# Two token blocks of a delta rule's inverse: each step of both issued back to back on TensorE

## What is computed

```python
m = jnp.where(strict, jnp.einsum('bhncd,bhnsd->bhncs', k_beta, kc) * decay, 0.0)
lmat = m + jnp.eye(CHUNK, dtype=m.dtype)
rhs = jnp.concatenate([v_beta, k_beta * jnp.exp(gc)[..., None]], axis=-1)
sol = lax.linalg.triangular_solve(lmat, rhs, left_side=True, lower=True, unit_diagonal=True)
```

## Time and profile before

| | us |
|---|---|
| median of 3 runs | 905.12 |
| the three runs | 903.41, 905.12, 905.43 |
| profiled execution: its time | 902.75 |
| profiled execution: its span | 901.1 |
| TensorE busy in the span | 882.1 |
| VectorE busy | 554.5 |
| ScalarE busy | 294.9 |

### The profile page before, as it was taken

The page is one execution under the profiler, slowest core; times in us unless marked ns, Lnnn a source line. Parts: engine busy times, 40 slices in busy tenths (PEclk is TensorE's granted clock), DMA queues, the critical chain, the costliest instruction groups (busy, mean ns, idle before and its releaser), DMA issues.

```text
span 901.1 us, 13501 instructions
## 1 busy us (share of the span) xinstructions
PE 882.1 (98%) x4615; PEld 705.7 (78%) x4615; DVE 554.5 (62%) x978; ACT 294.9 (33%) x598; POOL 72.7 (8%) x138
## 2 busy tenths in 40 slices
PE   9999999899999999999999999999999999898998
PEld 7887766688888888888888888888787776567877
DVE  6267557365877777777643343497788373774645
ACT  6245475523322222222210011263340213444710
POOL 0010000000010011000001100000000000000000
PEclk9999999999999999999999999999999999999999
DMA  8767433254766555556565566578456222221554
GB/s 277 239 211 226 139 121 113 97 161 139 238 200 195 186 186 191 195 196 197 196 189 187 189 197 199 180 263 266 145 169 192 95 74 92 71 94 47 186 184 145
DMA packets 53862, 154.74 MB, mean 172 GB/s; under 512 B 9628, under 2 KB 15020, under 8 KB 53688
## 3 DMA queue, kind: packets, MB, share of 16 engines
q1 hardware_dynamic: 24496, 75.84, 26.7%
q0 software_dynamic: 19008, 69.21, 23.7%
q10 hardware_dynamic: 10312, 9.06, 3.2%
HBM read 149.60 MB, written 4.49 MB: 171 GB/s over the span
## 4 chain that ended last, share of the span: by engine, by line
PE 89%; DMA 4%; DVE 3%; ACT 2%; issue 2%; POOLq 0%; SPq 0%; ACTq 0%; DVEq 0%
PE bank L716 77%; DMA HI<-wstream 3%; PE bank L1193 1%; PE bank L1171 1%; PE bank L891 1%; PE bank L877 1%; DVE LO L1736 1%; DMA RAW<-wstream 1%; PE bank L1085 1%; PE bank L1102 1%; PE bank L901 1%; ACT SQO L1669 1%; PE bank L1182 1%; PE bank L757 0%; PE bank L1041 0%
## 5 line engine op out<-in xcount | busy, mean ns | idle before, releaser
L716 PE MATMUL bank<-GH,HI 128*128 128x512 f32 x708 | 286.8, 405 | 0.0
L716 PE MATMUL bank<-GH,LO 128*128 128x512 f32 x708 | 275.8, 390 | 0.0
L716 PE MATMUL bank<-GL,HI 128*128 128x512 f32 x708 | 275.4, 389 | 0.0
L1736 DVE TENSOR_TENSOR LO<-RAW,HI 128x1024 fp32r<-128x1024 f32 x86 | 105.2, 1223 | 109.5 <-DMA HI<-wstream 107.5
L716 PEld LDWEIGHTS bank<-GH,HI 128*128 128x128 f32 x708 | 133.3, 188 | 36.7 <-issue 9.1
L716 PEld LDWEIGHTS bank<-GH,LO 128*128 128x128 f32 x708 | 133.0, 188 | 28.4
L716 PEld LDWEIGHTS bank<-GL,HI 128*128 128x128 f32 x708 | 133.4, 188 | 23.1
L698 POOL DMA_DIRECT2D HI<-wstream x132 | 70.1, 531 | 804.3 <-PE bank L716 786.2
L1441 ACT ACTIVATE YC<-AB,PAR 128x512 f32<-128x512 f32 x44 | 36.0, 817 | 140.7 <-DVE AB L1923 140.7
L716 PE MATMUL bank<-AH,HI 128*128 128x512 f32 x176 | 68.5, 389 | 0.0
L716 PE MATMUL bank<-AL,HI 128*128 128x512 f32 x176 | 68.5, 389 | 0.0
(11 more groups left out here) (322 smaller groups left out, 1156.1 us busy)
## 6 DMA issues: line engine op xcount, KB each, us to landing
RAW<-wstream SPq DMA_DIRECT2D x135, 512.0 KB, 3.7
HI<-wstream POOLq DMA_DIRECT2D x132, 512.0 KB, 4.9
X<-x_t SPq DMA_DIRECT2D x8, 256.0 KB, 7.5
NCB<-out_t ACTq DMA_DIRECT2D x8, 256.0 KB, 3.6
out_t<-X ACTq DMA_DIRECT2D x8, 256.0 KB, 5.6
XR<-out_t ACTq DMA_DIRECT2D x8, 256.0 KB, 4.2
out_t<-XR SPq DMA_DIRECT2D x7, 256.0 KB, 3.2
EG<-out_t ACTq DMA_DIRECT2D x1, 1024.0 KB, 4.8
```

Of the source, the lines that this page charges most:

```text
L716: mm = pe.matmul(out, a, b, start=(first and n == 0), stop=(last and n == 2))
L1736: dve.tensor_tensor(LO[:, u % RING, :], RAW[:, u % RING, :], HI[:, u % RING, :].bitcast(F32), ALU.subtract).then_inc(unit_split, 1)
```

## The change

The groups that `_prepare` hands to `_spread` are other ones. Before, nearly each group held one step of one block, so that fills stood behind each step. After, a group holds the same step of both blocks of the pair, one behind the other, and the fills that stood behind each stand behind both. At level 4 Z and X form one group, and X at level 5 and Y at level 6 form one, with both blocks' X ahead of both blocks' Y. A pair thus has eight groups in place of sixteen. The set of items is the same, and no function of an engine is changed.

```diff
+def _both(b, *steps):
+
+    return [(what, (x, l)) for what, l in steps for x in (b, b + 1)]
+
+
 def _prepare(b, fills):
...
-    steps = [[("Y", (x, 4))] for x in (b, b + 1)] + [[("Z", (x, 4)), ("X", (x, 4))] for x in (b, b + 1)]
-    steps += [[(what, (x, l))] for l in LEVELS[1:] for what in ("Y", "Z", "X") for x in (b, b + 1)]
-    steps += [[("W", b)], [("W", b + 1)]]
+    steps = [_both(b, *level) for level in ([("Y", 4)], [("Z", 4), ("X", 4)], [("Y", 5)], [("Z", 5)],
+                                            [("X", 5), ("Y", 6)], [("Z", 6)], [("X", 6)])]
+    steps.append([("W", b), ("W", b + 1)])
     return inputs + _spread(steps, fills)
```

## The result

The changed kernel takes 898.4 us in the median (10 runs, 897.11 to 901.88) against 904.0 us for the kernel before (10 runs, 901.94 to 905.43), a ratio of 0.9949 with a 95% interval of 0.9935 to 0.9963. The profiled execution takes 897.82 us (span 896.1) where its own sum gave 898.95. A second comparison gave 898.35 us against 902.22 and a ratio of 0.9955 (0.9940 to 0.9970). Of all runs in this document three stood far apart from the others of their kernels (1444 and 3524 us of the kernel before, 1454 us of one experiment); ratios and intervals are without them.

A forecast was written before the change was run, and what follows sets the result against it. TensorE, busy 98% of the span, was taken as the bound. Savings of 4.05 us less 0.25 of waits gave 898.95 us for the profiled execution; the median 905.12 less 3.8 gave 901.3, range 899.8 to 903.6.

The forecast's parts named there:

- a join of two 64x32 steps: Y and Z steps at levels 4 and 5 of both pairs: seven joins at 0.32 us save 2.24 us.
- Y5 of the second pair: Two Y steps at level 5, with the key spread between them before: 1.96 us becomes 1.59, saving 0.37 us.
- each X5 and Y6 run: X5, X5, Y6, Y6 in one run: 2.52 us becomes 2.21, saving 0.31 us in each of both pairs.
- the Z6 pair: Joining the Z steps at level 6 of the second pair saves 0.33 us; the first pair's stand joined already.
- the X6 pair: Joining the X steps at level 6 of the second pair: 1.08 us becomes 0.80, saving 0.28 us.
- The waits: New waits of TensorE for VectorE in the inverse, tightest at Z4 of the second pair: 0.25 us, from 0 to 0.5.
- The end: Behind the inverse: HI's issue moves from 754.17 to near 750.3, the gap to the span's end stays 147 us.
- The step that failed: Whole kernel: the median of three runs, 905.12 us, 2.4 above the profiled execution, less 3.8 us gives 901.3.
- 1, the joint is not free: Second of two joined steps waits for a drain, 0.58 us not 0.47; 1.3 us lost, 902.6 us; chance 0.13.
- 2, backlog: VectorE's backlog at Z(2,4) does not move forward; the first pair's 1.8 us is waited away, 903.1 us; chance 0.07.
- 3, no change: Attention starts at a time set by HI's transfer, which does not come earlier; 905.1 us; chance 0.09.
- 4, VectorE can't serve two blocks: Second joined step finds VectorE's input 0.6 us late; ten joins cost 6.0 us against 3.8, 907.3 us; chance 0.05.

## Why the prediction was right in its mechanism and missed its range

**The sum.** 4.05 us were forecast before waits; the stretch fell by 4.14. By parts, the first pair 1.84 against 1.8, the second 2.2 to 2.3 against 2.25. The terms read from rows of before held to some hundredths of a microsecond each: a join of two 64x32 steps 0.32 as forecast, Y5 of the second pair 0.33 for 0.37, each X5 and Y6 run 0.38 for 0.31, the Z6 pair 0.34 for 0.33, the X6 pair 0.31 for 0.28. The Z6 pair, which stood joined already, had the price of a join in it.

**The waits.** 0.25 us were taken, 0 were found: the VectorE waits at Z(2,4) didn't come, since the backlog moved forward with TensorE as argued, and the product was done 0.17 us before Z(2,4) needed it. That TensorE would wait there if one piece of cover were missing, two experiments show.

**The end.** The issue of HI after unit 7 and VectorE's remainder behind it, GpSimd's and VectorE's timelines of the changed kernel beside the earlier trace rows:

```profile
750.94 0.53 POOL L703 DMA_DIRECT2D HI<-wstream  x1 [10.61 <-PE bank L721]
...
755.60 1.22 DVE L1741 TENSOR_TENSOR LO<-RAW,HI 128x1024 fp32r<-128x1024 f32 x1 [3.30 <-DMA HI<-wstream]
```

The issue comes 3.23 us earlier and the remainder 3.28, which is the inverse's 4.14 less the 0.9 by which the whole inverse began later. So the gain went through the transfer, as argued. The distance from the issue to the end was forecast unchanged at 147 us and is 145.2. That is the one sign that failed. In these two traces it is 1.62 us of clock in the scan, less the 0.5 at 768, and 0.6 of a transfer; nothing shows that the change did it.

**The step that failed** is the last one, "The median of the three runs is 2.4 us above that execution, 905.12; less 3.8 us it gives 901.3 us". Up to there the working gave 898.95 us for one execution, and 898.4 was measured as the median. The 2.4 us put on top came from three runs that had all come out slow. The kernel before has a median of 904.0 in the ten runs of the same comparison and 902.2, 903.2 and 902.7 in the three later ones, and of its 76 later runs only 8 took 905.12 us or more. So the base was 2 to 3 us too high, 1.1 of which shows in the first comparison itself. From 902.2 to 903.2 us the forecast gain of 3.8 gives 898.4 to 899.4, and the 4.14 that the stretch lost give 898.1 to 899.0. From the 904.0 of the same comparison they would give 900.2 and 899.9, so some 1.5 us of its difference of 5.6 are not the inverse's. The gain itself was 0.34 us too small in the forecast, 0.25 of it the waits that did not come.

The range was wrong with the base, for it gave the median of few runs 0.6 us either way, where the three runs shown already lay 2 us apart and the profiled one below all of them. What that spread goes with is shown: runs of one kernel differ by 1.6 to 2.2 us between a mean clock of 0.998 and of 0.996. That the three were slow ones was bad luck; to lay a forecast of 0.4% on them was not. The ratio forecast, 901.3 / 905.12 = 0.9958, lies inside both measured intervals.

**The rivals.** 1, the joint is not free: out, 1.05 us for 32 records, no drain between; the semaphore tail that the Trainium skill states (TensorE: Matmul & The Clock Gate, "The cost: per-tile semaphore tail") isn't visible either, as the second sixteen records add 0.47 us (1.05 for 32, 0.58 for 16), which is sixteen times the pitch of 0.029 with nothing over. 2, backlog: out. 3, no change: out, as the issue of HI came 3.23 us earlier. 4, VectorE can't serve two blocks: not with two pieces of cover, yes with one or none (0.18 to 1.4 us a join).

**What stays open.** The medians of the first comparison lie 5.6 us apart and the inverse accounts for 4.1; the interval of the ratio, 3.3 to 5.9 us, holds both, and the clocks of that comparison's runs of the kernel before are not on record. Why the low clock falls on one execution and not on the next is not settled by these runs.

## What to carry to other kernels

Small matmuls in 64x64 tiles between full-array ones cost 0.32 us each time for the change of form, on top of their own time, and TensorE counts as busy meanwhile; put steps of one form together, and look for a pair that stands joined already to read the price from. Keep behind each joined pair as much other work as the next engine needs for both (two pieces, 1.4 us, here), since an uncovered wait of 0.18 to 1.4 us soon takes more than the 0.32 that a join saves. And take the base for a forecast of 0.4% from many runs, with their granted clocks beside them.

## What the runs showed of the hardware that was not expected

A wait of TensorE of 1.2 us, laid between small matmuls in a stretch that was otherwise full, was followed both times by microseconds at a granted clock of 0.50 (1.2 GHz), with dense matmuls at a pitch of 0.43 us in place of 0.23; it more than doubled the price of the wait. The same idle 2.02 us in the scan was followed by the low clock in four of eleven traces (the first of before among them, and not the first of the changed kernel), at the same work. Without that idle time (the norm moved behind, two kernels) 4 of 11 runs were at a mean clock of 1.0; of the 155 runs of all kernels that have it, 10 were.

Tiled matmuls between full-array ones started 0.33 us behind the last of these in place of 0.23, and the next one's start stood 0.33 to 0.34 ahead of the one after it (0.31 behind full-array transposes), with 32 columns (64x64 tiles) as with 128 and 512 (64x128 tiles), and the profile counts it as busy time of TensorE. Full-array float32 steps set apart between dense float32r pieces cost nothing in the sum (57.89 us with them apart, 57.93 together).
